# Sums of squares of the differential heads from a rounded high and low part

## The chip, the core and the metric

The kernel runs on one core of a Trainium2 chip. The metric is the device time of one launch in microseconds (us). Five things work side by side on the core: TensorE (PE, matrix products; its weight loads are shown apart as PEld), VectorE (DVE), ScalarE (ACT), GpSimd (POOL), and SyncE (SP), which issues the DMAs that bring the weights. Each engine executes its own list in order and waits on semaphores where it needs what another one makes.

## What is computed

Four layers of a first block (pooling, gated convolution, latent attention, pooling), then two layers of a second block, on 512 tokens of width 1024 in fp32. Each layer of the second block has eight stick-breaking heads of width 64 and four differential heads of width 128; so there are eight differential heads in the program. A differential head takes two softmaxes, subtracts one from the other and is then normalised over its own 128 channels:

```
def rmsnorm(x, g):
    xf = x.astype(jnp.float32)
    y = xf * lax.rsqrt(jnp.mean(xf * xf, axis=-1, keepdims=True) + EPS) * g.astype(jnp.float32)
...
        p = jax.nn.softmax(jnp.where(allowed, s, neg), axis=-1)
        attn = p[:, :, 0] - lam * p[:, :, 1]
...
        df_out = (rmsnorm(df_heads, subln_norm[l]) * (1.0 - lambda_init)).reshape(B, S, DF_WIDTH)
        mixed = jnp.concatenate([sb_out, df_out.astype(sb_out.dtype)], axis=-1)
        x = x + jnp.einsum('bse,ed->bsd', mixed, w_o[l])
```

The change concerns the mean of squares inside this `rmsnorm`.

## The kernel before

Activations lie channels by tokens: a tile of 128 partitions (channels) by 512 columns (tokens). A product in the kernel is made of fp32r operands: a value is stored as a rounded high part (suffix h) and the remainder (suffix l), and a product is three matmuls, high by high, low by high and high by low (`mm3`, L416 to L418). ACT makes the high parts (`high`, L1027; weights L1018), DVE the low parts (`low`, L1644; weights L1636), and in the second block POOL those of most weights (L2419, four instructions of 256 columns to a weight tile of 1024).

Each engine has a program of its own (`pe_program`, `act_program`, `dve_program`, `pool_program`, `sp_program`), and in the second block (`second_layer`) its order is a list of calls written out by hand, in which stick-breaking heads 0 to 7, differential heads 0 to 3, projections and the output projection `wo` are interleaved. Nothing reorders it. Results of PE lie in eight banks of PSUM (`ps`). In these layers the list `LAYER_BANKS` says which bank each result takes, and PE waits before it takes one until its last reader has marked it free (`psfree`).

A differential head h ends like this. ACT copies its output into OB and squares it into the tile ACC (`df_out`). DVE adds to ACC a term that stands for epsilon (`df_eps`, four instructions at L2173), marked `accd`. PE sums over the 128 channels with a product by a matrix of ones (`df_squares`, which calls `sum_squares`): for these heads one fp32 matmul, L452. ACT takes the inverse root out of the sum with Ln and Exp (`root`, L1048 and L1056), and its Ln frees the bank. DVE scales OB (`df_norm`, L2182), and ACT and DVE split it into YH[4 + h] and YL[4 + h] (`df_high`, `df_low`), which `wo` reads. Before that the same YH and YL tiles hold rotated queries and keys of heads (`dqk`).

`sum_squares` has a second form, which is used for five norms of the whole width (`SUMS_SPLIT`): the sum is rounded into a high part by ACT and a low part by DVE, and PE multiplies each by ones in fp32r (L446 and L447).

Around the four sums the lists read as follows. In PE's list `df_squares(0)` stands between the projections dq 2 and dq 3; `df_squares(1)` between the projection dk 3 and `sb_pv(3)`; `df_squares(2)` between `wo(0, 1)` and `sb_scores(6)`; `df_squares(3)` between `sb_scores(7)` and `sb_pv(6)`, which is followed by `wo(1, 2)`. `df_exp(h, ...)` are the exponentials of ACT for a differential head (L1167), `soft(h)` those for a stick-breaking head (ACT L1364, L1368, L1372; DVE L2101, L2104), `keep(h)` is the split of soft's result, which `sb_between(h)` multiplies, and `df_sums(h)` (first instructions L2145) prepares on DVE the join of the two softmaxes. In `LAYER_BANKS` the sum of head 3 takes bank 0, and the next result that takes bank 0 after it is `wo(1, 2)`.

Of the kernel before, what the change touches and what calls it, by code (L numbers as in the profile page):

```python
# [65 lines left out]
SUMS_SPLIT = (1, 2, 3, 5, 7)  # L66
# [30 lines left out]
class Counts:  # L97
# [14 lines left out]
    def at(self, *result):  # L112
        if self.known is None:
            return "act", 0
        return self.known[result]
# [171 lines left out]
def program(nc, D, out):  # L287
    ctx = ExitStack()
    with ctx:
# [6 lines left out]
        YH = [sb(f"yh{i}", S, F32R) for i in range(8)]  # L296
        YL = [sb(f"yl{i}", S, F32R) for i in range(8)]
# [83 lines left out]
            return 0.8 - 0.6 * math.exp(-0.3 * l)  # L381

        def sum_parts(use):
            return (PTH[:, 0:S], PTL[:, 0:S]) if use == 2 else (DFH[:, 0:S], DFL[:, 0:S])

        def last_square(use):
# [7 lines left out]
        def pe_program(handle, c):  # L394
# [44 lines left out]

            def sum_squares(use):  # L440
                b = bank("rs", use)
                if use in SUMS_SPLIT:
                    pe.wait_ge(*at("ones"))
                    pe.wait_ge(*at("suml", use))
                    h, lo = sum_parts(use)
                    pe.do.matmul(b[:, :], onesr[:, :], h, start=True, stop=False)  # L446
                    pe.do.matmul(b[:, :], onesr[:, :], lo, start=False, stop=True).then_inc(  # L447
                        *mark("group", ("mm", "rs", use)))
                    return
                pe.wait_ge(*at(*last_square(use)))  # L450
                pe.wait_ge(*at("const"))
                pe.do.matmul(b[:, :], ones, ACC[:, :], start=True, stop=True).then_inc(  # L452
                    *mark("group", ("mm", "rs", use), ("accfree", use)))
# [545 lines left out]
        def act_program(handle, c):  # L999
# [21 lines left out]
            def taking(*key):  # L1021
                weights(unit[key] + LOOK)
# [291 lines left out]
            def second_layer(l, done):  # L1314
# [33 lines left out]
                def turned(nm, h):  # L1348
                    swap(l, nm, h, ps(nm, l, h), ("mm", nm, l, h))
# [9 lines left out]
                def soft(h):  # L1359
                    if h:  # L1360
                        act.wait_ge(*at("bpl", l, h - 1, 0))
                    for kbs, k0, n in GR:
                        act.wait_ge(*at("mm", "ss", l, h, kbs[0]))
                        act.do.activation(SA[:, k0:k0 + n], ps("ss", l, h, kbs[0])[:, 0:n], ACT.Abs).then_inc(  # L1364
                            *mark("act", ("abs", l, h, kbs[0])))
                    for kbs, k0, n in GR:
                        act.wait_ge(*at("abs", l, h, kbs[0]))
                        act.do.activation(SA[:, k0:k0 + n], SA[:, k0:k0 + n], ACT.Exp, scale=-1.0).then_inc(  # L1368
                            *mark("act", ("sexp", l, h, kbs[0])))
                    for kbs, k0, n in GR:  # L1370
                        act.wait_ge(*at("sexp", l, h, kbs[0]))
                        act.do.activation(SA[:, k0:k0 + n], SA[:, k0:k0 + n], ACT.Ln, bias=1.0).then_inc(  # L1372
                            *mark("act", ("soft", l, h, kbs[0])))
# [7 lines left out]
                def weights_of(h):  # L1381
                    act.wait_ge(*at("mm", "sb", l, h, 0))
                    for kbs, k0, n in GR:
                        act.wait_ge(*at("logw", l, h, kbs[0]))
                        act.do.activation(SA[:, k0:k0 + n], SA[:, k0:k0 + n], ACT.Exp).then_inc(
                            *mark("act", ("wexp", l, h, kbs[0])))
                        high(SBH[:, k0:k0 + n], SA[:, k0:k0 + n], ("wexp", l, h, kbs[0]), ("bph", l, h, kbs[0]))
# [8 lines left out]
                def df_exp(h, base):  # L1396
                    qbs = DF_QBS[base]
                    if h:
                        act.wait_ge(*at("mm", "tp", l, h - 1, 2))
                    blocks = []  # L1400
                    for qb in qbs:
                        for m in range(2):
                            n = 128 * (qb + 1)
                            src = ps("ds", l, h, 0 if qb == 1 else qb, m)
                            c0 = 128 if qb == 1 else 0
                            blocks.append((src[:, c0:c0 + n], (GA, GB)[m][:, OFF[qb]:OFF[qb] + n]))
                    free = [("psfree", "ds", l, h, qb, m) for qb in qbs if qb != 1 for m in range(2)]
                    exps(blocks, base, 0.125, ("neg", l, h, base)).then_inc(*mark("act", ("exp", l, h, base), *free))
# [4 lines left out]
                def df_out(h):  # L1413
# [6 lines left out]
                        *mark("act", ("oc", l, h), ("psfree", "pv", l, "d", h)))  # L1420
                    square(("df", l, h), 0, OB[:, :], ("oc", l, h))

                def df_root(h):
                    root(("df", l, h), 128, True)

                def df_high(h):
                    if h in (1, 2):
                        act.wait_ge(*at("mm", "ds", l, h + 1, 16))
                    high(YH[4 + h][:, :], OB[:, :], ("on", l, h), ("yh", "wo", l, 4 + h))

                act.wait_ge(*at("lamsum", l))
# [56 lines left out]
                soft(3)  # L1488
                df_exp(1, 32)
                df_exp(1, 16)  # L1490
                taking('dq', l, 3)
                turned("dq", 2)
                df_root(0)
# [15 lines left out]
                soft(4)  # L1509
                df_exp(2, 32)  # L1510
                df_exp(2, 16)
                turned("dk", 3)
                df_root(1)
                keep(4)
# [14 lines left out]
                taking('wo', l, 0, 0)  # L1529
                plain("sk", 3)  # L1530
                df_exp(3, 16)
                weights_of(5)
                df_root(2)
                taking('wo', l, 0, 1)
# [6 lines left out]
                df_out(3)  # L1541
                taking('wo', l, 0, 3)
                weights_of(6)
                df_root(3)
                soft(7)
                df_high(3)
                keep(7)
                taking('wo', l, 1, 0)
# [62 lines left out]
        def dve_program(handle, c):  # L1611
# [400 lines left out]
            def second_layer(l):  # L2012
# [69 lines left out]
                def plain(nm, k):  # L2082
                    o = 0 if nm == "sq" else 2
                    low(sqk(k)[o + 1][:, :], temp("pj", l, nm, k), sqk(k)[o][:, :],
                        ("plh", l, nm, k), ("pl", l, nm, k), ("tfree", "pj", l, nm, k))
# [82 lines left out]
                def df_eps(h):  # L2168
# [4 lines left out]
                        t = dve.do.scalar_tensor_tensor(a, ident, sc(48 + 4 * (h % 2), qb), a, ALU.mult, ALU.add)  # L2173
                    t.then_inc(*mark("dve", ("accd", l, h)))

                def df_turn(h):
                    turn_low(DFL, DFH, (l, h))

# [9 lines left out]
                def wo_add(m):  # L2188
                    if l == 0:
                        dve.wait_ge(*at("x", 4, m))  # L2190
                    add_out(m, ("wo", l, 0, m), ("xwo", l, m))
# [49 lines left out]
                df_eps(0)  # L2241
                df_max(1, 16)
                soft(3)
                df_sums(1)
                df_join(1)
                turned("dq", 2)
# [16 lines left out]
                df_max(2, 16)  # L2263
                df_eps(1)
                soft(4)
                df_sums(2)
                df_join(2)
                turned("dk", 3)
# [19 lines left out]
                between(5)  # L2288
                plain("sq", 3)
                plain("sk", 3)  # L2290
                df_sums(3)
                df_join(3)
                weights_of(5)
# [9 lines left out]
                weights_of(6)  # L2303
                df_eps(3)
                wo_add(5)
                wo_add(3)
                wo_add(6)
                df_norm(3)
                soft(7)
                keep(7)  # L2310
                df_low(3)
                between(7)
# [515 lines left out]
```

## Time and profile before

| | |
|---|---|
| time, median of 3 runs | 2710.25 us (2709.89 to 2710.47) |
| profiled execution, span from first to last instruction | 2708.0 us |
| PE busy | 2687.0 us, 99% of the span |
| DVE, ACT, POOL busy | 1551.6, 1154.0, 681.2 us |
| chain that ended last | PE 91%, DVE 4%, POOL 2%, ACT 2% |
| mean granted clock of TensorE | 1.000 |

The median lies 2.25 us above the span of the profiled execution. Starts and durations of matmuls overlap in the trace: a row's duration is longer than the distance to the next row, and that distance is what a matmul costs in a dense stretch. The second block's layer 0 lies at some 1465 to 2085 us, and layer 1 repeats the pattern 616.9 us later.

### The profile page before, as it was taken

The page shows a single profiled execution, that of the slowest core. Times are in us where ns is not written, and L with a number is a line of the kernel's source. Part 1 is how long each engine was busy: PE and PEld are TensorE (multiplying, and loading weights), DVE is VectorE, ACT ScalarE, POOL GpSimd, SP SyncE. Part 2 cuts the span into 40 slices and gives each one's busy share as a digit, 9 for nine tenths or more (in the row PEclk, how much of TensorE's full clock was granted, in tenths as well). Part 3 has the DMA queues.
Part 4 walks back from the last instruction along what each step waited for, and adds up shares of the span by engine and source line. Part 5 has one row for each costly group of instructions (what it writes and reads, how often), then busy time and mean ns, then how long its engine had stood idle before and what let it go on. Part 6 is the DMA issues. An engine that isn't in the chain of part 4 may idle for free.

```text
span 2708.0 us, 32235 instructions
## 1 busy us (share of the span) xinstructions
PE 2687.0 (99%) x12902; PEld 2250.4 (83%) x12902; DVE 1551.6 (57%) x2312; ACT 1154.0 (43%) x1836; POOL 681.2 (25%) x695
## 2 busy tenths in 40 slices
PE   8999999999999999999999999999999999999999
PEld 7888888888888888888888888788888888788887
DVE  6656554344466646665575668644445558655444
ACT  4323423222347636532235767522224667522223
POOL 1000111011136626400004753411103553511100
PEclk9999999999999999999999999999999999999999
DMA  4332232323222222223322221233333211233332
GB/s 160 97 101 93 91 108 93 101 95 100 90 75 61 67 75 67 86 95 101 100 94 88 82 67 40 79 101 97 98 94 103 78 57 54 71 101 94 97 98 78
DMA packets 69414, 238.80 MB, mean 88 GB/s; under 512 B 7696, under 2 KB 10256, under 8 KB 69264
## 3 DMA queue, kind: packets, MB, share of 16 engines
q1 hardware_dynamic: 69264, 236.73, 28.1%
q8 instruction: 102, 1.67, 0.3%
q14 instruction: 48, 0.39, 0.0%
HBM read 234.60 MB, written 2.10 MB: 87 GB/s over the span
## 4 chain that ended last, share of the span: by engine, by line
PE 91%; DVE 4%; POOL 2%; ACT 2%; issue 0%; DMA 0%; SPq 0%; ACTq 0%; DVEq 0%
PE ps L416 29%; PE ps L418 29%; PE ps L417 29%; POOL wl L2419 2%; PE ps L552 1%; PE ps L777 1%; PE ps L776 1%; PE ps L485 0%; DVE wl L1636 0%; ACT wh L1018 0%; PE ps L613 0%; PE ps L612 0%; DVE xl L1648 0%; PE ps L470 0%; PE ps L452 0%
## 5 line engine op out<-in xcount | busy, mean ns | idle before, releaser
L1018 ACT ACTIVATE wh<-raw 128x1024 fp32r<-128x1024 f32 (+2 forms) x453 | 465.2, 1028 | 730.7 <-PE ps L418 723.7
L416 PE MATMUL ps<-xh,wh 128*128 128x512 f32 x1920 | 751.7, 391 | 0.2 <-POOL wl L2419 0.2
L418 PE MATMUL ps<-xh,wl 128*128 128x512 f32 x1920 | 747.4, 389 | 0.0
L417 PE MATMUL ps<-xl,wh 128*128 128x512 f32 x1920 | 747.2, 389 | 0.0
L1636 DVE TENSOR_TENSOR wl<-raw,wh 128x1024 fp32r<-128x1024 f32 (+1 forms) x339 | 447.7, 1321 | 156.9 <-ACT wh L1018 156.5
L416 PE MATMUL ps<-yh,wh 128*128 128x512 f32 x1088 | 425.3, 391 | 1.9 <-POOL wl L2419 1.9
L416 PEld LDWEIGHTS ps<-xh,wh 128*128 128x128 f32 x1920 | 360.5, 188 | 76.2 <-issue 1.0
L417 PE MATMUL ps<-yl,wh 128*128 128x512 f32 x1088 | 423.5, 389 | 0.0
L418 PE MATMUL ps<-yh,wl 128*128 128x512 f32 x1088 | 423.4, 389 | 0.0
L418 PEld LDWEIGHTS ps<-xh,wl 128*128 128x128 f32 x1920 | 360.4, 188 | 75.1
L417 PEld LDWEIGHTS ps<-xl,wh 128*128 128x128 f32 x1920 | 360.6, 188 | 74.8 <-issue 1.0
L2419 POOL TENSOR_TENSOR wl<-raw,wh 128x256 fp32r<-128x256 f32 x408 | 314.9, 805 | 323.2 <-ACT wh L1018 323.1
L2428 POOL TENSOR_TENSOR acc<-acc,t 128x512 f32<-128x512 f32 x59 | 83.3, 1413 | 715.6 <-ACT t L1039 713.3
L1673 DVE TENSOR_TENSOR x<-ps,x 128x512 f32<-128x512 f32 x152 | 104.4, 689 | 265.2 <-PE ps L418 265.2
L416 PEld LDWEIGHTS ps<-yh,wh 128*128 128x128 f32 x1088 | 204.3, 188 | 46.5 <-POOL wl L2419 3.9
L418 PEld LDWEIGHTS ps<-yh,wl 128*128 128x128 f32 x1088 | 204.2, 188 | 42.4
L417 PEld LDWEIGHTS ps<-yl,wh 128*128 128x128 f32 x1088 | 204.4, 188 | 41.6
L2613 POOL TENSOR_TENSOR t<-t 128x512 f32<-128x512 f32 x64 | 71.3, 1117 | 515.5 <-DVE t L2346 515.5
L1027 ACT ACTIVATE yh<-t 128x512 fp32r<-128x512 f32 x148 | 93.1, 631 | 170.6 <-POOL t L2613 58.6
L1644 DVE TENSOR_TENSOR yl<-t,yh 128x512 fp32r<-128x512 f32 x148 | 110.5, 747 | 83.3 <-ACT yh L1027 83.3
L1648 DVE SCALAR_TENSOR_TENSOR xl<-x,vec,xh 128x512 fp32r<-128x512 f32 x64 | 73.6, 1168 | 65.6 <-ACT xh L1029 65.6
L2346 DVE SCALAR_TENSOR_TENSOR t<-ps,r 128x512 f32<-128x512 f32 x64 | 44.2, 690 | 104.2 <-PE ps L418 103.9
(267 smaller groups left out, 3628.6 us busy)
## 6 DMA issues: line engine op xcount, KB each, us to landing
raw<-in_ff SPq DMA_DIRECT2D x120, 512.0 KB, 3.6
raw<-in_pool_in SPq DMA_DIRECT2D x64, 512.0 KB, 3.3
raw<-in_conv_in SPq DMA_DIRECT2D x64, 512.0 KB, 3.3
raw<-in_pool_out SPq DMA_DIRECT2D x32, 512.0 KB, 3.3
raw<-in_qk SPq DMA_DIRECT2D x32, 512.0 KB, 3.7
raw<-in_pool_grp SPq DMA_DIRECT2D x16, 512.0 KB, 3.3
raw<-in_conv_out SPq DMA_DIRECT2D x16, 512.0 KB, 3.3
raw<-in_mla_z SPq DMA_DIRECT2D x16, 512.0 KB, 3.6
```

Of the source, the lines that this page charges most:

```text
L416: pe.do.matmul(o, lh, rh_, start=start, stop=False)
L417: pe.do.matmul(o, lh, rl_, start=False, stop=False)
L418: return pe.do.matmul(o, ll, rh_, start=False, stop=stop)
L1018: act.do.activation(h[:, 0:ncol], r[:, 0:ncol], ACT.Copy).then_inc(*mark("whi", ("whi", k)))
L1027: act.do.activation(dst, src, ACT.Copy).then_inc(*mark("act", done))
L1636: dve.do.tensor_tensor(lo[:, 0:ncol], r[:, 0:ncol], f(h[:, 0:ncol]), ALU.subtract).then_inc(*mark("wlo", ("wlo", k)))
L1644: dve.do.tensor_tensor(dst, src, f(h), ALU.subtract).then_inc(*mark("dve", *done))
L1648: dve.do.scalar_tensor_tensor(dst, src, scale, f(h), ALU.mult, ALU.subtract).then_inc(*mark("dve", *done))
L1673: dve.do.tensor_tensor(x[m][:, :], ps(*key)[:, :], x[m][:, :], ALU.add).then_inc(*mark("dve", ("psfree",) + key, *done))
L2419: p = pool.do.tensor_tensor(lo[:, cc], r[:, cc], f(h[:, cc]), ALU.subtract)
L2428: pool.do.tensor_tensor(ACC[:, :], ACC[:, :], temp("sq", use, k), ALU.add).then_inc(*mark("pool", ("acc", use, k), ("tfree", "sq", use, k)))
L2613: pool.do.tensor_tensor(t, t, t, ALU.mult).then_inc(*mark("pool", ("ffs",) + key))
```

## The change

The sum of squares of each differential head is split into a high and a low part like those of the whole width, and multiplied as two fp32r products. The parts are kept in the head's own YH[4 + h] and YL[4 + h]. ACT gets `df_sum_high(h)`: a wait until the scores that still read that YH tile are done, then the rounding of ACC. DVE gets `df_sum_low(h)`, which makes the low part and marks `suml` and `accfree`. PE waits for `suml` in the place of `accd`. Besides, `soft(7)` is moved ahead of `df_root(3)` on ACT and ahead of `df_norm(3)` on DVE. The wait that stood in `df_high` moves into `df_sum_high`.

```diff
         def sum_parts(use):
+            if isinstance(use, tuple):
+                return YH[4 + use[2]][:, :], YL[4 + use[2]][:, :]
             return (PTH[:, 0:S], PTL[:, 0:S]) if use == 2 else (DFH[:, 0:S], DFL[:, 0:S])
...
                 b = bank("rs", use)
-                if use in SUMS_SPLIT:
+                if use in SUMS_SPLIT or isinstance(use, tuple):
...
+                def df_sum_high(h):
+                    act.wait_ge(*at("mm", "ds", l, (0, 2, 3, 3)[h], 16))
+                    high(YH[4 + h][:, :], ACC[:, :], ("accd", l, h), ("sumh", ("df", l, h)))
...
                 def df_high(h):
-                    if h in (1, 2):
-                        act.wait_ge(*at("mm", "ds", l, h + 1, 16))
...
                 df_exp(1, 16)
+                df_sum_high(0)
...
                 df_exp(2, 16)
+                df_sum_high(1)
...
                 df_exp(3, 16)
+                df_sum_high(2)
                 weights_of(5)
...
                 weights_of(6)
+                df_sum_high(3)
+                soft(7)
                 df_root(3)
-                soft(7)
                 df_high(3)
...
+                def df_sum_low(h):
+                    low(YL[4 + h][:, :], ACC[:, :], YH[4 + h][:, :], ("sumh", ("df", l, h)), ("suml", ("df", l, h)),
+                        ("accfree", ("df", l, h)))
...
                 soft(3)
+                df_sum_low(0)
                 df_sums(1)
...
                 soft(4)
+                df_sum_low(1)
                 df_sums(2)
...
                 plain("sk", 3)
+                df_sum_low(2)
                 df_sums(3)
...
                 wo_add(5)
+                df_sum_low(3)
                 wo_add(3)
                 wo_add(6)
+                soft(7)
                 df_norm(3)
-                soft(7)
                 keep(7)
```

On DVE, after `soft(3)` (the same after `soft(4)`), the low part now stands ahead of the reciprocals of `df_sums`. Before:

```order
L2101 SCALAR_TENSOR_TENSOR s<-ps,s 128x512 [waits s_act]
L2104 SCALAR_TENSOR_TENSOR s<-ps,s 128x512 [waits s_dve]
L2145 RECIPROCAL small<-small 128x1
L2145 RECIPROCAL small<-small 128x1 [waits s_act]
L2145 RECIPROCAL small<-small 128x2 [waits s_act]
```

and in the changed kernel (whose lines are numbered some places on):

```order
L2109 SCALAR_TENSOR_TENSOR s<-ps,s 128x512 [waits s_act]
L2112 SCALAR_TENSOR_TENSOR s<-ps,s 128x512 [waits s_dve]
L1652 TENSOR_TENSOR yl<-acc,yh 128x512 [waits s_act]
L2153 RECIPROCAL small<-small 128x1 x2
L2153 RECIPROCAL small<-small 128x2
```

The new third row is the low part of the sum; it waits for ACT's high part, and all of `soft` stands ahead of it.

On ACT, at head 3, the two instructions of `df_root(3)` stand in front of `soft(7)` before:

```order
L1027 ACTIVATE pth<-s 128x512 [waits s_act]
L1048 ACTIVATE t<-ps 128x512 [waits s_group]
L1056 ACTIVATE t<-t 128x512 [waits s_act]
L1364 ACTIVATE s<-ps 128x384 [waits s_dve]
L1364 ACTIVATE s<-ps 128x384
L1364 ACTIVATE s<-ps 128x512
L1368 ACTIVATE s<-s 128x384 [waits s_act] x2
L1368 ACTIVATE s<-s 128x512 [waits s_act]
L1372 ACTIVATE s<-s 128x384 [waits s_act] x2
L1372 ACTIVATE s<-s 128x512 [waits s_act]
L1027 ACTIVATE yh<-ob 128x512 [waits s_dve]
```

and in the changed kernel behind it:

```order
L1029 ACTIVATE pth<-s 128x512 [waits s_act]
L1029 ACTIVATE yh<-acc 128x512 [waits s_dve]
L1366 ACTIVATE s<-ps 128x384 [waits s_group] x2
L1366 ACTIVATE s<-ps 128x512 [waits s_group]
L1370 ACTIVATE s<-s 128x384 [waits s_act] x2
L1370 ACTIVATE s<-s 128x512 [waits s_act]
L1374 ACTIVATE s<-s 128x384 [waits s_act] x2
L1374 ACTIVATE s<-s 128x512 [waits s_act]
L1050 ACTIVATE t<-ps 128x512 [waits s_group]
L1058 ACTIVATE t<-t 128x512 [waits s_act]
L1029 ACTIVATE yh<-ob 128x512 [waits s_dve]
```

The Ln that frees the bank of the sum (L1048, now L1050) has moved behind nine instructions of `soft(7)`.

On PE one row becomes two and nothing else moves. At head 0 of layer 0, before:

```order
L418 MATMUL ps<-xh,wl 128x512
L452 MATMUL ps<-acc,const 128x512 [waits s_dve,s_act]
L416 MATMUL ps<-xh,wh 128x512 [waits s_wlop]
```

and in the changed kernel:

```order
L420 MATMUL ps<-xh,wl 128x512
L448 MATMUL ps<-yh,onesr 128x512 [waits s_dve,s_act]
L449 MATMUL ps<-yl,onesr 128x512
L418 MATMUL ps<-xh,wh 128x512 [waits s_wlop]
```

The wait on s_dve is in the same place, but for a later instruction of DVE.

## Rows read from the trace of the kernel before

**Rows 1.** The page: busy time by engine; shares of the chain that ended last.
```profile
PE 2687.0 (99%) x12902; PEld 2250.4 (83%) x12902; DVE 1551.6 (57%) x2312; ACT 1154.0 (43%) x1836; POOL 681.2 (25%) x695
...
PE 91%; DVE 4%; POOL 2%; ACT 2%; issue 0%; DMA 0%; SPq 0%; ACTq 0%; DVEq 0%
```

**Rows 2.** Timeline (start, duration in us, engine, line), PE: head 0's sum; a split sum.
```profile
1597.65 1.02 PE L452 MATMUL ps<-acc,const 128*128 128x512 f32 x2
...
1598.74 0.40 PE L417 MATMUL ps<-xl,wh 128*128 128x512 f32 x1
...
1752.32 0.39 PE L446 MATMUL ps<-pth,onesr 128*128 128x512 f32 x1
...
1752.79 0.39 PE L416 MATMUL ps<-xh,wh 128*128 128x512 f32 x1
```

**Rows 3.** Instructions on the tile acc: count, duration in ns (min/median/max), first and last start.
```profile
L1027 ACT ACTIVATE pth<-acc x5: 613/615/617, 319.7 to 2367.0; 128x512 fp32r<-128x512 f32 x5
L1644 DVE TENSOR_TENSOR ptl<-acc,pth x5: 677/684/685, 321.2 to 2368.3; 128x512 fp32r<-128x512 f32 x5
```

**Rows 4.** Timeline, ACT and DVE around head 0's sum: what follows the exponentials and soft(3).
```profile
1598.55 1.10 ACT L1018 ACTIVATE wh<-raw 128x1024 fp32r<-128x1024 f32 x1
...
1599.56 0.28 DVE L2145 RECIPROCAL small<-small 128x1 f32<-128x1 f32 x3
```

**Rows 5.** Timeline, PE, ACT and DVE around head 1's sum.
```profile
1634.11 1.02 PE L452 MATMUL ps<-acc,const 128*128 128x512 f32 x2
1635.36 0.50 PE L416 MATMUL ps<-pth,g 128*128 128x512 f32 x1 [0.23 <-ACT s L1167]
1635.70 0.39 PE L417 MATMUL ps<-ptl,g 128*128 128x512 f32 x1
...
1635.33 2.40 ACT L1154 ACTIVATE t<-ps 32x512 f32<-32x512 f32 x4
...
1636.79 0.28 DVE L2145 RECIPROCAL small<-small 128x1 f32<-128x1 f32 x3
```

**Rows 6.** Timeline, DVE and PE around head 2's sum.
```profile
1672.44 0.27 DVE L2145 RECIPROCAL small<-small 128x1 f32<-128x1 f32 x3
...
1673.80 0.38 PE L416 MATMUL ps<-g 64*128 64x256 f32 x1
```

**Rows 7.** Timeline, DVE, ACT and PE around head 3's sum.
```profile
1696.54 1.13 DVE L2173 SCALAR_TENSOR_TENSOR acc<-const,small,acc 128x128 f32<-128x128 f32 x4
...
1698.95 0.60 ACT L1048 ACTIVATE t<-ps 128x512 f32<-128x512 f32 x1 [3.25 <-PE ps L452]
...
1700.12 1.34 ACT L1364 ACTIVATE s<-ps 128x384 f32<-128x384 f32 x3
...
1704.04 0.63 ACT L1027 ACTIVATE yh<-ob 128x512 fp32r<-128x512 f32 x1
...
1698.98 0.40 PE L417 MATMUL ps<-ptl,g 128*128 128x512 f32 x1
...
1700.62 0.45 PE L416 MATMUL ps<-yh,wh 128*128 128x512 f32 x1
```

**Rows 8.** Timeline, PE: two waits for a weight's low part from POOL.
```profile
1652.56 0.33 PE L801 MATMUL ps<-yh,yl 64*128 64x384 f32 x1
1653.32 0.50 PE L416 MATMUL ps<-yh,wh 128*128 128x512 f32 x1 [0.43 <-POOL wl L2419]
...
1710.74 0.39 PE L418 MATMUL ps<-yh,wl 128*128 128x512 f32 x1
1711.65 0.50 PE L416 MATMUL ps<-yh,wh 128*128 128x512 f32 x1 [0.52 <-POOL wl L2419]
```

**Rows 9.** Timeline, DVE: where its list last waits for PE ahead of head 1's sum.
```profile
1617.07 0.69 DVE L2077 SCALAR_TENSOR_TENSOR t<-ps,r 128x512 f32<-128x512 f32 x1 [3.40 <-PE ps L418]
```

**Rows 10.** Waits of PE over the span: us in total, times, longest us.
```profile
PE ps L470 <- POOL wl L2419: 2.6, 2, 1.3
```

**Rows 11.** Timeline, PE: four matmuls of the kernel's opening.
```profile
11.94 1.91 PE L485 MATMUL ps<-xh,wl 128*128 128x512 f32 x4
```

## The prediction

> **What bounds the kernel now.** I read the shares of the page first, then the timeline of the four engines around the four sums of layer 0, and last the banks and the order of instructions of both kernels. PE is busy 99% of the span and holds 91% of the chain that ended last [rows 1]. So a microsecond that PE neither works nor waits is a microsecond of the whole, and a wait that is added to PE's list is paid in full, unless it replaces one that PE has further on. The reader is to see in the timeline, for each of the four sums, three times: when PE comes to the sum, when ACT is through with what stands ahead of the high part, and when DVE is through with what stands ahead of the low part. Layer 1 shows the same pattern 616.9 us later, so I work out layer 0 and double it.
>
> **What the matmuls give.** An fp32 sum is two records of PE from 1597.65, and the second matmul of what follows starts at 1598.74. The split sum takes 1752.79 - 1752.32 = 0.47 for two matmuls, 0.23 to 0.24 each, and 0.23 is the steady distance of all that have 512 columns. With it the fp32 sum has cost 1598.74 - 0.23 - 1597.65 = 0.86 [rows 2]. That is 0.39 less for each sum, 8 x 0.39 = 3.1 us for the whole, if nothing else were changed.
>
> **What the parts cost.** Each sum gets a high part on ACT of 0.615 us and a low part on DVE of 0.684 [rows 3], both of the same shape from the same tile as in the split that exists. ACT is busy 43% and DVE 57% of the span [rows 1], so their 8 x 0.62 = 5 us and 8 x 0.68 = 5.5 us of work cost nothing by their length. What costs is where they stand. PE used to wait for the epsilon term in ACC; now it waits for a low part that stands in DVE's list behind all of `soft` and behind a high part that ACT makes after all the exponentials of the next head.
>
> *Head 0.* ACT is through with the exponentials at 1598.55, where it goes on to a weight; the high part takes that place until 1598.55 + 0.62 = 1599.17. DVE is through with `soft(3)` at 1599.56, where the reciprocals start [rows 4]; the low part takes that place and ends at 1599.56 + 0.68 = 1600.24. PE comes to the sum at 1597.65 and now stands still to about 1600.30, some 2.6 us. A first matmul after a wait is followed by its second at about 0.33 (1635.36 to 1635.70 in [rows 5]), so the sum's second matmul starts at 1600.63, the two that follow at 1600.86 and 1601.09. The last of them stood at 1598.74 [rows 2]. **Shift 2.35 us.** Behind the waiting matmul PE has queued the projection dq 3, `sb_pv(2)` and all that follows; ACT and DVE wait for those.
>
> *Head 1.* The same order. ACT goes on at 1635.33, so the high part ends by 1635.95; DVE comes to the reciprocals at 1636.79, so the low part ends at 1637.47. PE comes at 1634.11 and stands still for 3.4 us, to 1637.53. The following matmuls start at 1637.86, 1638.09 and 1638.32; the last of these stood at 1635.70 [rows 5]. **Shift 2.6 us.** In this a short wait that PE had there for a bank (it ends at 1635.36) is already used up. Could head 0's standstill have let DVE get ahead, so that head 1's is smaller? DVE waits 3.40 us for PE at 1617.07 [rows 9], and from there to 1636.8 its list runs on without a pause; the wait moves with PE, and so the distance from PE to DVE at head 1 stays what it was.
>
> *Head 2.* DVE comes to the reciprocals at 1672.44 [rows 6]; the low part ends at 1673.12, PE's sum starts at 1673.18 and what follows it at 1673.74, where it stood at 1673.80. **Shift -0.05 us**: the gain of the shorter sum is eaten by a wait of a third of a microsecond. `weights_of(5)` on ACT and the join on DVE, queued behind the parts, come 0.6 and 0.7 later, under 5 us of PE's work before PE asks for them.
>
> *Head 3.* DVE ends the epsilon term at 1696.54 + 1.13 = 1697.67. The high part runs to 1698.3, the low part (behind `wo_add(5)`, which ends at that time too) to 1699.05, and the sum starts at 1699.1; `sb_pv(6)`'s second matmul stands at 1699.9 in the place of 1698.98, a shift of 0.9. From that row `sb_pv(6)` runs 1700.62 - 1698.98 = 1.64 to `wo(1, 2)`, so PE comes there at 1701.55 [rows 7]. But `wo(1, 2)` takes bank 0, that of the sum, and the Ln that frees it has moved behind `soft(7)`. `soft(7)` takes ACT 1704.04 - 1700.12 = 3.92; it starts after the high part at 1698.25 (an activation of that size holds its engine 0.54 to the next) and ends at 1702.17, and the Ln, 0.60 long, at 1702.77 [rows 7]. `wo(1, 2)` starts at 1702.83 instead of 1700.62. **Shift 2.2 us.** Before, the Ln ended at 1699.55, a microsecond ahead of PE. What `soft(7)` gains by the move, 1.9 us, goes to `keep(7)`; but that now waits for `df_norm(3)`, which DVE runs after its own part of `soft(7)`, and it comes out about where it was, at 1707.2 for the first part, with PE 2 us later. So no new wait there, and no gain.
>
> **What is given back.** A PE that is late doesn't wait at two places where POOL had been late. At 1653.32 the distance to the row ahead is 0.76 where 0.18 would do, at 1711.65 it is 0.91 where 0.23 would do [rows 8]: 0.58 + 0.68 = 1.26. POOL's own list is late by 0.7 at most at the first (through the high part on ACT and the low part on DVE), by some 1.0 at the second (its weight's tile is freed by PE), against a PE that is 2.6 and 2.2 late; so both waits go entirely. The longest wait of PE behind the opening, 1.3 us for POOL ahead of the first matmuls of the feed-forward part [rows 10], stays: POOL's list there starts from a weight tile that PE's last `wo` products free.
>
> **Sum.** Per layer 2.35 + 2.6 - 0.05 + 2.2 - 1.26 = 5.85, for two layers 11.7. The span goes from 2708.0 to 2719.7, and with the 2.25 us between span and median the time from 2710.25 to **2722 us**. About 0.2% (5.4 us) is what a measurement of this kernel can tell from no change, so this is slower.
>
> **Bounds.** The trace of before has no split sum whose parts stand ahead of PE's need, so how long PE stands still rests on the positions. Each of the three standstills may be off by 0.3 us through the time from one engine's end to another's start: 2 us for the whole. At least, if the second wait of head 3 were hidden, 1.3 per layer would go: 2719. At most, none of the 1.26 is given back: 2724.5.
>
> **Rivals.**
> *The clock falls.* PE would stand still 2.6 and 3.4 us, while its longest pause behind the opening is now 1.3 [rows 10]. In the opening, where it has had little to do, four matmuls of 512 columns span 1.91 us, against 3 x 0.23 + 0.39 = 1.08 later on [rows 11]: they are some 0.45 apart in the place of 0.23, TensorE at 1.2 and not at 2.4 GHz, though the column of the granted clock shows 1.00 there. If such a stretch followed each of the two standstills of head 1, it would cost half its length: 1 us each if it is as long as that row, 7 if as long as all the opening to 13.9. I take 3.5, half of the latter, 7 us in all: 2729. For it speaks that no pause of this length is in the trace behind the opening, so nothing shows that the clock stands it; against it, that the clock never fell after all the pauses up to 1.3. The Trainium skill, in "TensorE: Matmul & The Clock Gate", section "HAM oscillation — how this bites in real kernels", says that pauses of TensorE between bursts bring its clock back to the lower level, each time anew. The trace shows that only for the opening.
>
> *Not slower: the parts are ready in time.* If ACT and DVE had run so far ahead that the low part ended before 1597.65 at head 0 and before 1634.11 at head 1, PE would keep its 3.1 us: 2707, within the bound of no change. The point from which it decides is the place of the low part: it had to end 2.6 and 3.4 us earlier. The rows speak against it, since `soft` on DVE ends after PE's arrival at both, and the epsilon term alone could be read earlier, as it was.
>
> *Made up later.* A late PE meets more that is ready than I count: the wait of 1.3 per layer for POOL [rows 10] goes as well, and head 3's second wait is hidden. That takes 2 x (1.3 + 1.3) = 5.2 off: 2716.8, just above the bound. Against it speaks that POOL's list there starts from PE, and that `soft(7)` is one piece of ACT's list.
>
> **How the numbers follow.** My case, 2717.5 to 2726, has 0.70. The clock has 0.09 (2726 to 2733), made up later 0.12 (2713 to 2719, a third of it within 0.2%), not slower 0.08 (2705 to 2712), a gain of over 0.2% by what I don't see 0.01. So slower 0.87, same 0.12, faster 0.01. The range that holds 8 in 10 reaches from 2715, into the case of made up later, to 2728, into that of the clock.
>
> **What would show it.** In the profile after, the timeline of PE should show L448 (the sum's first matmul) with an idle time of about 2.6 us behind DVE's low part at head 0, 3.4 at head 1, 0.3 at head 2 and 1.3 at head 3; then 1.3 of idle before the first matmul of `wo(1, 2)` behind ACT's Ln; no wait for POOL at the two places. Busy time of ACT should rise by 5 us, that of DVE by 5.5. Matmuls at 0.43 apart after head 1's sum would say the clock. No idle before L448 would say that I misread DVE's list, and the whole would fall.

## The result, and the profile after

The changed kernel takes 2725.84 us (median of 4 runs, 2725.22 to 2728.07) against 2710.24 for the one before: ratio 1.006 with an interval of 1.0046 to 1.0074, 15.6 us slower. The forecast was 2722 in a range of 2715 to 2728. The sign holds, and so do the standstills behind it; a quarter to a third of the slowdown comes from falls of TensorE's clock, which the sum doesn't hold.

First the page of the profile after: busy time by engine, and the chain that ended last. The busy times answer to the first of [rows 1].

```profile
PE 2692.9 (99%) x12902; PEld 2258.5 (83%) x12902; DVE 1557.5 (57%) x2320; ACT 1157.6 (42%) x1844; POOL 676.6 (25%) x695
...
PE 91%; DVE 4%; ACT 2%; POOL 1%; issue 0%; DMA 0%; SPq 0%; ACTq 0%; DVEq 0%
```

The span has grown by 16.2 us, from 2708.0 to 2724.2, PE's busy time by 5.9, though its sums have become shorter. The rest is waiting. DVE's busy time has risen by 5.9 and ACT's by 3.6, where the forecast had 5.5 and 5. The waits of PE over the span (us in total, times, longest):

```profile
PE ps L448 <- DVE small L2153: 9.3, 6, 2.6
...
PE ps L448 <- ACT s L1366: 2.8, 2, 1.4
...
PE ps L418 <- ACT t L1050: 1.1, 1, 1.1
...
PE ps L418 <- DVE g L1652: 0.6, 2, 0.3
PE ps L418 <- POOL wl L2435: 0.3, 1, 0.3
```

L448 is the first product of a sum. It waits eight times, 12.1 us in all. (The engine named is the one whose semaphore event came last by the profile; what PE waits for is the low part just ahead of the reciprocals.) The waits for POOL at the two places of [rows 8] are gone in both layers; the 0.3 that is left is at another place. PE's list around the four sums of layer 0:

```profile
1596.90 0.39 PE L420 MATMUL ps<-xh,wl 128*128 128x512 f32 x1
1599.88 0.48 PE L448 MATMUL ps<-yh,onesr 128*128 128x512 f32 x1 [2.59 <-DVE small L2153]
1600.19 0.57 PE L449 MATMUL ps<-yl,onesr 128*128 128x512 f32 x1
1600.57 0.63 PE L418 MATMUL ps<-xh,wh 128*128 128x512 f32 x1
1600.99 0.63 PE L419 MATMUL ps<-xl,wh 128*128 128x512 f32 x1
...
1640.81 0.47 PE L448 MATMUL ps<-yh,onesr 128*128 128x512 f32 x1 [1.80 <-DVE small L2153]
...
1678.53 0.47 PE L448 MATMUL ps<-yh,onesr 128*128 128x512 f32 x1 [0.25 <-DVE small L2153]
...
1704.57 0.47 PE L448 MATMUL ps<-yh,onesr 128*128 128x512 f32 x1 [1.40 <-ACT s L1366]
...
1708.26 0.47 PE L418 MATMUL ps<-yh,wh 128*128 128x512 f32 x1 [1.12 <-ACT t L1050]
```

And what head 0's sum waits for, on ACT and DVE, which answers to [rows 4]:

```profile
1598.03 0.67 ACT L1029 ACTIVATE yh<-acc 128x512 fp32r<-128x512 f32 x1
...
1598.45 0.69 DVE L2112 SCALAR_TENSOR_TENSOR s<-ps,s 128x512 f32<-128x512 f32 x1
1599.06 0.68 DVE L1652 TENSOR_TENSOR yl<-acc,yh 128x512 fp32r<-128x512 f32 x1
```

The low part starts when `soft(3)` is done and ends at 1599.74; PE goes on at 1599.88. The idle times 2.59, 0.25, 1.40 and 1.12 are those of the forecast (2.6, 0.3, 1.3, 1.3). Head 1 has 1.80 where 3.4 was forecast. And the distances behind head 0's sum are wrong for the clock that was taken: 1600.19 to 1600.57 to 1600.99, 0.4 us for a matmul where 0.23 is the steady distance. The table of windows of this kernel shows why. Each row is a stretch of time: the busy time and the instructions of each engine in it, then the mean granted clock of TensorE (PEclk, 1.00 for 2.4 GHz, 0.50 for 1.2), then two columns on DMA:

```profile
core 0: us, PE busy (x) PEld busy (x) DVE busy (x) ACT busy (x) POOL busy (x), PEclk, DMA share, GB/s
1597.00:1604.00 7.00, 4.41 (x13) 3.32 (x12) 6.93 (x15) 6.23 (x14) 4.04 (x5) 0.76 0.10 13
1604.00:1630.00 26.00, 25.71 (x142) 21.70 (x141) 16.29 (x30) 15.28 (x28) 12.10 (x11) 1.00 0.17 58
1630.00:1635.00 5.00, 5.00 (x25) 3.84 (x24) 4.34 (x16) 4.94 (x12) 0.00 (x0) 0.66 0.00 0
1635.00:1641.00 6.00, 4.20 (x19) 3.22 (x18) 5.86 (x19) 5.93 (x19) 0.00 (x0) 1.00 0.00 1
...
2224.00:2228.00 4.00, 3.79 (x10) 3.00 (x11) 4.00 (x11) 3.58 (x6) 3.94 (x5) 0.61 0.01 4
2255.00:2259.00 4.00, 4.00 (x21) 3.22 (x20) 3.93 (x14) 3.97 (x10) 0.00 (x0) 0.58 0.00 0
2265.00:2269.00 4.00, 3.87 (x15) 3.54 (x15) 4.00 (x14) 1.96 (x4) 1.78 (x1) 0.61 0.02 6
2330.00:2334.00 4.00, 3.52 (x11) 3.06 (x12) 2.86 (x6) 4.00 (x9) 0.00 (x0) 0.59 0.01 2
```

The clock fell to its lower level, 1.2 in the place of 2.4 GHz, six times in this execution, four times right behind a standstill: at head 0 of both layers and at heads 1 and 3 of layer 1. The two others start at 1631 and 2256, 31 us behind the standstill of head 0, and some 3 us behind a wait of only 0.29 us: that for DVE ahead of `sb_scores(4)`, at 1628.24 and 2252.57. In the profiled execution of before its mean was 1.000. So the rival "the clock falls" came in, on top of the forecast standstills.

### The profile page after: what moved, and what is told of

It reads as the page before. It is cut to its first block, busy times and chain, and to the rows that moved or that the text cites. A ratio compares the mean times of both kernels' runs of the same rounds, so it can differ in the third digit from the quotient of the medians.

```text
span 2724.2 us, 32251 instructions
## 1 busy us (share of the span) xinstructions
PE 2692.9 (99%) x12902; PEld 2258.5 (83%) x12902; DVE 1557.5 (57%) x2320; ACT 1157.6 (42%) x1844; POOL 676.6 (25%) x695
## 4 chain that ended last, share of the span: by engine, by line
PE 91%; DVE 4%; ACT 2%; POOL 1%; issue 0%; DMA 0%; SPq 0%; ACTq 0%; DVEq 0%
PE ps L418 29%; PE ps L419 29%; PE ps L420 29%; POOL wl L2435 1%; PE ps L554 1%; PE ps L779 1%; PE ps L778 1%; PE ps L487 0%; DVE wl L1644 0%; DVE small L1831 0%; ACT wh L1020 0%; DVE ptl L1652 0%; PE ps L615 0%; PE ps L614 0%; DVE xl L1656 0%
```

## The experiments

The kernels were timed in three sets, each on one chip together with the kernel before, whose medians were 2709.94, 2710.03 and 2710.03 us; so kernels of different sets can be compared to about 0.1 us.

**The parts alone.** The changed kernel, without the move of `soft(7)`, and with the old product:

```diff
-                if use in SUMS_SPLIT or isinstance(use, tuple):
+                if use in SUMS_SPLIT:
...
+                done = [] if isinstance(use, tuple) else [("accfree", use)]
                 pe.do.matmul(b[:, :], ones, ACC[:, :], start=True, stop=True).then_inc(
-                    *mark("group", ("mm", "rs", use), ("accfree", use)))
+                    *mark("group", ("mm", "rs", use), *done))
```

> All eight sums are split by ACT and DVE at the places of the changed kernel, but TensorE still multiplies ACC in fp32 and waits only for the epsilon term as before; soft(7) is not moved. Standstill theory (the time is lost because TensorE waits for parts that stand late in DVE's list): TensorE asks for nothing new, so 2710 to 2712. Added work theory (5 us more on ACT and 5.5 us more on DVE push their chains, which hold 6% of the chain that ended last): part of the 10.5 us shows, 2715 or more.

Measured: 2712.27 us (2711.76 to 2714.5), ratio 1.0008 (0.9999 to 1.0017). The 8 high and 8 low parts are there, and of the 15.6 us at most 2.3 come with them. That they push the engines' chains by 5 us or more is out. They aren't quite free, though. The wait of PE for DVE ahead of `sb_scores(4)` has grown from 0.62 to 1.07 in both layers:

```profile
1624.61 0.38 PE L418 MATMUL ps<-g 64*128 64x256 f32 x1 [1.07 <-DVE g L1653]
```

and in its profile the clock fell once in the stretch behind, in layer 0. Layer 1, where no fall lies, still took 1.1 us longer than before from the end of `sb_scores(3)` to the start of the feed-forward part: 0.5 of it up to `sb_scores(4)`, 0.6 from there to `sb_scores(5)`.

**Work in the place of the standstill.** Matmuls without use ahead of the sums, into the bank that the sum overwrites:

```diff
                     pe.wait_ge(*at("ones"))
+                    for _ in range((11, 14, 0, 5)[use[2]] if isinstance(use, tuple) else 0):
+                        pe.do.matmul(b[:, :], onesr[:, :], XH[0][:, :], start=True, stop=True)
                     pe.wait_ge(*at("suml", use))
```

> The changed kernel, with 11, 14, 0 and 5 matmuls without use (512 columns each, 0.23 us) put into TensorE's list ahead of the sums of heads 0, 1, 2 and 3 of each layer, into the bank that the sum then overwrites: TensorE works for 2.5, 3.2 and 1.1 us where it stood still. If the granted clock fell because TensorE stood still, its record shows 1.00 in these stretches, and the time is that of the standstills alone, 2721 to 2723. If the falls have another cause, they stay (six in the profiled execution of the changed kernel) and the time stays at 2725 to 2727.

Measured: 2722.01 us (2721.17 to 2722.31), 3.8 us under the changed kernel, with 60 matmuls more. Its windows at the same places, and in layer 1 the wait for DVE ahead of `sb_scores(4)`:

```profile
1597.00:1604.00 7.00, 7.00 (x31) 5.49 (x30) 6.93 (x15) 6.37 (x15) 4.08 (x5) 1.00 0.09 7
1604.00:1630.00 26.00, 25.70 (x151) 21.57 (x149) 17.41 (x32) 16.80 (x31) 12.10 (x11) 1.00 0.19 60
1630.00:1635.00 5.00, 5.00 (x25) 4.05 (x24) 4.93 (x20) 5.00 (x13) 0.00 (x0) 1.00 0.00 0
...
2249.14 0.38 PE L418 MATMUL ps<-g 64*128 64x256 f32 x1 [0.30 <-DVE g L1654]
...
2252.00:2256.00 4.00, 4.00 (x20) 3.15 (x19) 3.97 (x15) 3.97 (x10) 0.00 (x0) 0.57 0.00 0
```

The four falls behind standstills are gone, so these come from the standstills. Of the two others one is gone and one is left: it starts at 2252.2, 3.1 us behind the wait for DVE ahead of `sb_scores(4)`, as the one at 2256 did in the changed kernel (3.0 us behind). So this experiment doesn't put the falls of that stretch down to the standstills. Other traces speak against it: in the kernel of the next experiment the clock held there in both layers, though the standstills were in place, and with the parts earlier, further down, it fell there in both, without a standstill at head 0.

The time, 2722.0, is that of the forecast, 2722, but it isn't quite free of falls: the one that is left makes head 1's part of layer 1 1.3 us longer than that of layer 0.

**`soft(7)` back behind the root.** The changed kernel with

```diff
                 df_sum_high(3)
-                soft(7)
                 df_root(3)
+                soft(7)
                 df_high(3)
```

and the same for `df_norm(3)` on DVE.

> The changed kernel with soft(7) back behind df_root(3) on ACT and behind df_norm(3) on DVE. Bank theory (wo(1, 2) waits for the Ln that frees the sum's bank, which the move has put behind 3.9 us of soft(7)): the wait before wo(1, 2) goes, 1.3 us per layer less, 2722.5 to 2724. If the move was needed to keep soft(7) and sb_between(7) in time: the same or more, 2726 or above.

Measured: 2726.21 us (2723.68 to 2728.18). The median lies where the rival had it, at 2726 or above, but it doesn't decide: the runs reach from 2723.68, which was the bank theory's case, to 2728.18, at a mean clock of 0.996 to 0.997. The profile tells more. The wait for L1050 is gone, and there are six falls, each during a standstill or within 1 us of its end; all six cost time, against four in the changed kernel. It also shows head 1 as forecast, 3.34 us where no fall lies ahead:

```profile
1641.46 0.47 PE L448 MATMUL ps<-yh,onesr 128*128 128x512 f32 x1 [3.34 <-DVE small L2153]
```

In the changed kernel the fall at 1631 had made PE late, and took 1.5 us out of this wait: a fall that lies ahead of such a wait costs next to nothing.

**The same with the clock held.** The two edits together:

> The kernel of e2_filled (so the clock should hold) with soft(7) back behind df_root(3) and df_norm(3), as in e3_root_first. Bank theory: the wait of 1.2 us before wo(1, 2) goes in each layer, of which 1.2 to 1.3 us come off: 2719 to 2720.5 against 2722.0, and no wait for L1052 in TensorE's list. If soft(7) is needed that early: 2722 or more.

Measured: 2720.56 us (2720.39 to 2721.02), 1.45 less than with `soft(7)` moved. The wait before `wo(1, 2)` is gone; of its 1.2 us per layer 0.6 come off in the trace (head 3's part goes from 1.51 to 0.94 in layer 0, from 1.49 to 0.93 in layer 1), since the next wait for POOL is back, as in [rows 8]:

```profile
1715.74 0.50 PE L418 MATMUL ps<-yh,wh 128*128 128x512 f32 x1 [0.53 <-POOL wl L2437]
```

The bank theory holds; I had expected the whole of the wait and forgotten what my own sum says of POOL. The rest of the 1.45 isn't shown to come from the edit: the profiled execution of this kernel is 0.6 us ahead at the end of `sb_scores(3)` of layer 0, in work that both share.

**`soft(7)` moved alone**, in the kernel before:

> The kernel before with one part of the change alone: soft(7) ahead of df_root(3) on ACT and of df_norm(3) on DVE. No sum is split. Bank theory: the Ln that frees bank 0 ends 2.8 us later, at 1702.4, TensorE waits 1.8 us before wo(1, 2) and gets 0.7 back at its next wait for POOL: 1.1 to 1.2 us per layer, 2712 to 2712.8. If the move helps as such (keep(7) and sb_between(7) earlier): 2710 or less.

Measured: 2712.72 us (2710.68 to 2714.05), ratio 1.0009 (1.0000 to 1.0018). The wait is there in both layers:

```profile
1702.42 0.47 PE L416 MATMUL ps<-yh,wh 128*128 128x512 f32 x1 [1.61 <-ACT t L1048]
```

In the trace PE is at 1697.26 at the end of `sb_scores(7)`, where it was at 1697.25, and starts the feed-forward part at 1733.52 in the place of 1732.52: 1.0 us of a layer from this part of the change, and nothing gained by it. In layer 1 this part takes 0.97. The medians differ by 2.7. For the 0.7 that is left the trace has falls of the clock in the stretch behind `sb_scores(4)`, in both layers.

**Parts earlier.** The changed kernel with the parts of heads 0 and 1 ahead of exponentials and `soft`:

```diff
                 soft(3)
+                df_sum_high(0)
                 df_exp(1, 32)
                 df_exp(1, 16)
-                df_sum_high(0)
...
                 df_max(1, 16)
+                df_sum_low(0)
                 soft(3)
-                df_sum_low(0)
...
                 df_max(2, 32)
-                df_max(2, 16)
                 df_eps(1)
+                df_max(2, 16)
+                df_sum_low(1)
                 soft(4)
-                df_sum_low(1)
```

> The changed kernel with the parts of heads 0 and 1 made earlier: the high part ahead of the exponentials of the next head, the low part ahead of soft on DVE, and at head 1 the epsilon term ahead of the last maxima. Place theory: no standstill at head 0, under 1 us at head 1 (then a bank that the delayed exponentials free), and no fall of the clock there; 2712 to 2715. If the standstill came from the length of the parts and not their place: 2720 or more.

Measured: 2714.77 us (2713.94 to 2715.9). Eleven of the 15.6 us go by the place of the parts of two heads per layer, with their number and length unchanged. No wait for L448 is left at heads 0 and 1, and no fall right behind these sums. But the expectation that the clock holds between these heads missed: its mean was 0.996 in the profiled execution and 0.998 in the others. It fell at head 3's standstills and, in both layers, in the stretch behind `sb_scores(4)`, here that of layer 0, where PE had waited 0.71 us for DVE:

```profile
1627.00:1631.00 4.00, 4.00 (x19) 3.23 (x20) 3.97 (x14) 3.97 (x10) 0.00 (x0) 0.57 0.00 0
```

**The wait alone.** The kernel before, with a wait ahead of two of its fp32 sums and nothing else:

```diff
                 def df_squares(h):
+                    if h < 2:
+                        pe.wait_ge(*at("rec", l, h + 1, 34))
                     sum_squares(("df", l, h))
```

> The kernel before, with one thing added: TensorE waits, ahead of the sums of heads 0 and 1 in each layer, for DVE's first reciprocal of the next head (L2145, which stood at 1599.56 and 1636.79), that is about until where the parts were ready in the changed kernel less one instruction. No part is made, no product split, nothing moved on ACT or DVE. Standstill theory: 2.0 and 2.8 us of standstill per layer, some 0.9 of it given back at the waits for DVE at 1625 and for POOL at 1653: 7 to 8 us in all, and if such pauses make the clock fall without any help of the parts, 2 to 5 us on top: 2719 to 2723, with a mean clock of 0.997 to 0.998. If the parts' work had a share in either: 2717 or less, with the clock at 1.0 or 0.999.

Measured: 2721.77 us (2718.44 to 2722.52), mean clock 0.998. A wait without any part and any product does it, and it brings the clock down as well. The first wait of layer 0, 1.97 us, left the clock alone; the same wait in layer 1, 1.98 us, came with a fall, and PE lost 3.56 us in that part in the place of 1.91. Behind head 1's wait of layer 0, 2.7 us, the second and third of these windows show the fall:

```profile
1597.00:1604.00 7.00, 5.03 (x21) 3.51 (x20) 6.93 (x15) 5.98 (x15) 4.06 (x5) 1.00 0.11 23
...
1635.00:1641.00 6.00, 3.27 (x9) 1.64 (x8) 5.90 (x18) 4.54 (x15) 1.56 (x1) 0.80 0.00 1
1641.00:1645.00 4.00, 4.00 (x21) 3.44 (x20) 2.97 (x6) 2.73 (x6) 2.24 (x3) 0.88 0.02 4
```

**The product alone.** The filled kernel with the same wait for the parts, then one fp32 product of ACC in the place of the pair:

> The kernel of e2_filled, with the parts made and waited for, but the sum then taken as one fp32 product of ACC (0.86 us) in the place of the pair (0.47 us): measures the product alone. By the rows 0.39 us per sum where TensorE goes straight on, eight sums: 2722.0 + 3.1 = 2725.1; at head 3 part of it falls into the wait for the bank, so 2724.3 to 2725.1. If the two products cost as much as the one: 2722.

Measured: 2723.18 us (2722.07 to 2725.78), 1.2 over the filled kernel, where 2.3 to 3.1 were expected. The two traces give more. From the end of `sb_scores(3)` to the start of the feed-forward part PE takes 1.24 us longer in layer 0, and 0.42, 0.43 and 0.39 of it at heads 0, 1 and 2; at head 3 it falls into the wait for the bank (0.80 in the place of 1.20). In layer 1 it is 0.37 at head 0 and 0.35 at head 2. So a pair is some 0.4 us shorter, as read, and five of eight can be seen, 2.0 us. The sixth, head 1 of layer 1, is hidden by the clock: the filled kernel has its one fall there, and this kernel has none in the second block, so its layer 1 is 0.2 us shorter on the whole. Besides, this profile was 0.5 us ahead at the start of the second block, in work that both kernels share. That is how the two profiled executions come to differ by 0.6 us alone; why the medians differ by 1.2 isn't shown.

**Only where it can be had.** From all this a version: only heads 0 and 2 are split, the kernel before otherwise.

```diff
                 soft(3)
+                df_sum_high(0)
                 df_exp(1, 32)
...
                 plain("sk", 3)
+                df_sum_high(2)
                 df_exp(3, 16)
...
                 df_max(1, 16)
+                df_sum_low(0)
                 soft(3)
...
                 between(5)
+                df_sum_low(2)
                 plain("sq", 3)
```

> The kernel before, with only the sums of heads 0 and 2 split, their high parts ahead of the next exponentials and their low parts ahead of soft(3) and of plain(sq, 3), so that they are ready before TensorE asks; heads 1 and 3 and soft(7) as before. Place theory: no standstill, 4 sums x 0.39 = 1.6 us less, 2708.4 (2707.5 to 2710), if no other wait of TensorE grows by the 0.6 us that the parts push their engines. Rival: the parts push DVE's chain, and a wait of TensorE takes the gain: 2710 to 2712.

Measured: 2710.76 us (2708.14 to 2711.54), ratio 1.0000 (0.9991 to 1.0009). No sum waits, and no gain. Its runs fall apart by their mean clock: 2708.1 to 2708.7 at 0.999 (three), 2709.9 to 2711.5 below (eight). The profiled one belongs to these. PE's wait for DVE ahead of `sb_scores(4)` and the windows behind it:

```profile
1623.55 0.38 PE L421 MATMUL ps<-g 64*128 64x256 f32 x1 [0.76 <-DVE g L1655]
...
1622.00:1625.00 3.00, 2.25 (x17) 1.92 (x17) 2.23 (x5) 2.94 (x9) 0.00 (x0) 1.00 0.01 3
1625.00:1628.00 3.00, 3.00 (x20) 2.25 (x18) 2.37 (x6) 2.94 (x7) 0.00 (x0) 0.65 0.00 0
1628.00:1631.00 3.00, 3.00 (x7) 2.38 (x8) 2.93 (x13) 3.00 (x8) 0.00 (x0) 0.50 0.00 0
```

In 1628 to 1631 PE got through 7 matmuls.

**The same, with that wait filled** by three matmuls without use:

```diff
+                    if h == 4:
+                        b = use(sb_banks[0], ("ss", l, h, GR[0][0][0]))
+                        for _ in range(3):
+                            pe.do.matmul(b[:, :], onesr[:, :], XH[0][:, :], start=True, stop=True)
                     pe.wait_ge(*at("pl", l, "sq", p))
```

> The kernel of e7_early_02 with three matmuls without use (512 columns, 0.7 us) where TensorE waits 0.76 us for DVE ahead of sb_scores(4), a stretch in which the granted clock fell in its profile and in those of e1, e4 and e9. If that wait brings on the falls: they go from there, and the gain of the four shorter sums shows, 2708.2 to 2709. If the falls come from the stretch as a whole (transposes, products of 64 rows) or by chance: 2710 to 2711 again.

Measured: 2708.61 us (2707.77 to 2709.89), 2.15 us under the same kernel without the matmuls, of which there are three in each layer. Its windows:

```profile
1622.00:1625.00 3.00, 3.00 (x20) 2.26 (x18) 2.82 (x6) 2.20 (x6) 0.00 (x0) 1.00 0.26 105
1625.00:1628.00 3.00, 3.00 (x22) 2.47 (x23) 1.74 (x4) 2.90 (x7) 0.00 (x0) 1.00 0.00 0
1628.00:1631.00 3.00, 3.00 (x21) 2.44 (x20) 2.97 (x12) 3.00 (x8) 0.00 (x0) 1.00 0.00 0
```

The 21 matmuls of the last window hold small ones, which the kernel without the fill had behind it by then; the clean sign is the distance of those with 512 columns, 0.23 us from one to the next, against 0.43 there. No run had a mean clock under 0.999, where eight of eleven had without the fill. Against the kernel before it is 1.4 us, ratio 0.9995 with an interval of 0.9986 to 1.0003: the lowest median of all, and not clear of no difference.

**The three matmuls in the kernel before:**

> The kernel before with the same three matmuls as in e11, nothing else. If the wait brings on falls in some of its runs (its times reach from 2709.3 to 2712.7 at a mean clock of 1.000 to 0.998), they narrow to 2709.5 to 2710.3 at 1.000; if not, no difference from before.

Measured: 2709.59 us (2708.31 to 2710.07, ratio 0.9997, 0.9988 to 1.0006), all eleven runs at a mean clock of 1.000. Of the 21 runs of before eight were at 1.000, nine at 0.999 and four at 0.998, three of these four above 2711. So even the kernel before, whose profiled execution shows no fall, seems to have had them in some runs, and this wait of 0.6 us to have brought them on. It isn't shown: no trace of the kernel before holds such a fall, and the 0.44 us between the medians lie within the interval. The filled version with heads 0 and 2 split is another 1.0 us below; four shorter sums were to give 1.6.

## Why the prediction was right, and where it was not

The table follows PE from one stick-breaking head to the next. Each entry is the time by which PE fell behind the kernel before in that part, from the starts of the last three matmuls of `sb_scores(3)` to `sb_scores(7)` and the first of the feed-forward part, in the traces:

| part of a layer | forecast | filled, layer 0 | filled, layer 1 | after, layer 0 | after, layer 1 |
|---|---|---|---|---|---|
| head 0's sum | 2.35 | 2.01 | 2.04 | 3.72 | 3.71 |
| head 1's sum | 2.6 | 2.47 | 3.81 | 2.54 | 4.14 |
| wait for POOL, head 2's sum | -0.63 | -0.41 | -0.37 | -0.38 | -0.36 |
| head 3's sum, `wo(1, 2)`, wait for POOL | 1.5 | 1.50 | 1.49 | 1.51 | 1.66 |
| sum | 5.85 | 5.57 | 6.97 | 7.39 | 9.15 |

- *PE holds the chain, a wait added to it is paid.* Right: shown by the wait alone.
- *What the matmuls give*, 0.39 a sum: right, 0.35 to 0.43 between the traces of the two filled kernels.
- *The parts cost nothing by their length*: nearly. With the parts alone the kernel was 2.3 us slower, at an interval that reaches no change, and its layer 1, without a fall, took 1.1 us longer, half of it in a longer wait for DVE. In the filled kernel, where PE comes later, nothing of it shows: its layer 0 is shorter than forecast.
- *Head 0*: the standstill was 2.59 for 2.6. The shift is 0.34 smaller than forecast, since PE's wait for DVE ahead of `sb_scores(4)`, at 1625.06 before, went from 0.62 to 0.30. The prediction doesn't name this wait among those that give something back.
- *Head 1*: 3.34 in the kernel with the root ahead, for 3.4. *Head 2*: 0.25, for a third of a microsecond. *Head 3*: 1.40 and 1.12 to 1.20, for 1.3 and 1.28. `soft(7)` moved alone cost 1.0 per layer where 1.1 to 1.2 were expected.
- *What is given back*: right for the waits of [rows 8]; both went in both layers, and one came back when the standstill was taken away. The part with the first of them and head 2's sum gave back 0.36 to 0.41 where 0.63 was forecast; this wasn't followed.
- *The sum*: 11.7, against 12.1 measured in the filled kernel (2722.01 - 2709.94, at 60 matmuls more). That it comes so near is in part luck: its trace loses 5.57 in layer 0 and 6.97 in layer 1, of which 1.3 are the fall at 2252. Twice the layer without a fall is 11.1.
- *The clock* is the step that failed: the sum has nothing for it. I gave it 0.09 as a case of its own, and for its price I took half of the opening's length, 3.5 us a fall. In layer 0 after and filled differ at head 0 by 3.72 - 2.01 = 1.71: that is what one fall costs where PE works without a pause behind it (1.65 with the wait alone, 3.56 - 1.91). Over both layers the profiled execution loses 16.54 where twice 5.57 is 11.14: 5.4 us more, from four falls that count (three at 1.7, one at head 3 of which most went into the wait for the bank) and two that fell into waits. The Trainium skill, "TensorE: Matmul & The Clock Gate", section "HAM oscillation — how this bites in real kernels", stands behind this rival; on this point the trace agrees in part: the clock came down behind four of the six pauses of 1.4 us and more and, with work in their place, behind none. It wasn't each time.
- *The range* held the result by luck as well: 2725.84 lies 0.2 us under the bound of 2726 between my case and that of the clock, though it is made like the latter, the standstills and falls on top. What kept it so low is that a fall cost 1.7 us and not 3.5.

What stays open: what in the stretch of `sb_scores(4)` brings the clock down, and why only at times. In the eleven traces in which PE waits there for DVE, it fell there in 11 of 22 layers, from 1.7 to 3.1 us behind the wait: in 7 of the 10 with a wait of 0.6 to 1.1 us, and in 4 of the 12 with one of 0.3. With the wait filled, in two kernels, it fell in none of 4. The stretch also holds transposes and products of 64 rows; no run here changed those. Nor was it followed why the parts alone lengthened the wait for DVE to 1.07.

## What to carry to other kernels

Before a product is made cheaper by splitting its operand, look in the lists of the engines that make the parts for the last instruction that stands ahead of them, and compare its end with the time at which TensorE asks: here 0.4 us a sum was bought with standstills of 2.6 and 3.4. A reordering is checked by what it frees late, too: nine instructions moved ahead of an Ln held a PSUM bank for 2.8 us longer. Where TensorE has to wait anyway, count the clock in, and try whether matmuls without use in that place pay.

## What the runs showed of the hardware

- In the second block of these traces all eight waits of PE of 2.6 us and more came with a stretch at 1.2 GHz, and so did seven of the twelve from 1.39 to 1.98 us; those of 1.40, 1.61 (twice), 1.80 and 1.97 us did not. Such a stretch cost 1.7 us where dense work followed.
- In a stretch of small products the clock fell behind 7 of 10 waits of 0.6 to 1.1 us and behind 4 of 12 of 0.3. With three matmuls of 512 columns without use in the place of the wait it fell behind none of 4, and the kernel with heads 0 and 2 split became 2.15 us faster. In the kernel before they held the mean clock at 1.000 in each of eleven runs, whose times span 1.8 us; without them 21 runs span 4.0.
- Sixty matmuls without use made a kernel 3.8 us faster.
